# Three plain tiles share the input tiles as they come, and the first combined weights and inputs are made in another order

## What is computed

```python
def rms_norm(x, gain):
    y = xf * lax.rsqrt(jnp.mean(xf * xf, axis=-1, keepdims=True) + NORM_EPS)
    return (y * gain.astype(jnp.float32)).astype(x.dtype)

def swiglu(xn, w_in, w_out):          # 1024 -> 2 x 2816 -> 1024
    gate, up = jnp.split(xn @ w_in, 2, axis=-1)
    return (jax.nn.silu(gate) * up) @ w_out

x = first_block(x, ...)      # FFN 0, two-branch attention, FFN 1, then a norm of the result
x = second_block(x, ...)     # FFN 2, stick-breaking attention, FFN 3
# in either block: x = x + 0.5 * swiglu(rms_norm(x, n1), wi1, wo1), mixer, the same again
```

## Time and profile before

| | |
|---|---|
| median of 3 runs | 2038.31 us (2038.15 to 2039.38) |
| profiled execution, its own time | 2038.09 us |
| its span | 2036.3 us |
| mean granted clock of PE | 0.996 |
| instructions in the trace | 33055 |

### The profile page before, as it was taken

One profiled execution on the slowest core, in us unless ns is written; L12 is line 12 of the kernel. 1 busy time (PEld: TensorE's weight loads), 2 busy tenths in 40 slices (PEclk: granted clock), 3 DMA queues, 4 the chain that ended last, 5 costly groups with the idle time before them and its releaser, 6 DMA issues. The chain is left out here.

```text
span 2036.3 us, 33055 instructions
## 1 busy us (share of the span) xinstructions
PE 2014.3 (99%) x12322; PEld 1769.7 (87%) x12322; DVE 1285.5 (63%) x2245; ACT 1068.1 (52%) x1767; POOL 1074.5 (53%) x704
## 2 busy tenths in 40 slices
PE   9999999999999999999998999999999998999999
PEld 6998998777778889989987998998878877998997
DVE  8752765667762577626767764665688867752762
ACT  6652654344443466525656652653677755642651
POOL 2764775433322448646744774775322335764863
PEclk9999999999999999999999999999999998999999
DMA  4232323322121223332232333333444422332322
GB/s 170 94 107 90 110 96 117 137 83 73 63 73 62 93 83 107 108 109 94 92 106 79 111 102 104 100 100 115 115 136 125 132 86 73 104 114 83 108 98 96
DMA packets 69086, 206.18 MB, mean 101 GB/s; under 512 B 8448, under 2 KB 9472, under 8 KB 68928
## 3 DMA queue, kind: packets, MB, share of 16 engines
q1 hardware_dynamic: 67520, 201.29, 30.2%
q10 hardware_dynamic: 1408, 2.78, 0.4%
HBM read 189.49 MB, written 2.10 MB: 94 GB/s over the span
## 5 line engine op out<-in xcount | busy, mean ns | idle before, releaser
L622 POOL TENSOR_TENSOR w_lo<-raw,w_hi 128x1024 fp32r<-128x1024 f32 (+2 forms) x232 | 471.8, 2043 | 693.0 <-ACT w_hi L1240 528.3
L1240 ACT ACTIVATE w_hi<-raw 128x512 fp32r<-128x512 f32 (+2 forms) x472 | 359.1, 765 | 313.9 <-PE ps L698 250.9
L633 POOL TENSOR_TENSOR w_lo<-s,w_hi 128x512 fp32r<-128x512 f32 x234 | 312.1, 1335 | 184.8 <-ACT w_hi L1240 183.1
L770 PE MATMUL ps<-t_hi,w_hi 128*128 128x256 f32 x1248 | 353.9, 284 | 2.6 <-DVE scratch L1922 2.2
L771 PE MATMUL ps<-t_lo,w_hi 128*128 128x256 f32 x1248 | 353.5, 283 | 0.0
L772 PE MATMUL ps<-t_hi,w_lo 128*128 128x256 f32 x1248 | 353.5, 283 | 0.0
L633 POOL TENSOR_TENSOR w_lo<-raw,w_hi 128x512 fp32r<-128x512 f32 x234 | 301.7, 1303 | 69.0 <-ACT w_hi L1240 68.9
L696 PE MATMUL ps<-xn_hi,w_hi 128*128 128x512 f32 x648 | 262.3, 405 | 10.3 <-issue 5.4
L770 PE MATMUL ps<-xn_hi,w_hi 128*128 128x256 f32 x936 | 265.3, 283 | 1.5 <-POOL w_lo L633 1.5
L772 PE MATMUL ps<-xn_hi,w_lo 128*128 128x256 f32 x936 | 265.1, 283 | 0.0
L771 PE MATMUL ps<-xn_lo,w_hi 128*128 128x256 f32 x936 | 265.1, 283 | 0.0
(11 more groups left out here) (259 smaller groups left out, 3779.5 us busy)
## 6 DMA issues: line engine op xcount, KB each, us to landing
raw<-weights SPq DMA_DIRECT2D x294, 512.0 KB, 3.3
raw<-weights SPq DMA_DIRECT2D x68, 256.0 KB, 2.8
raw<-weights SPq DMA_DIRECT2D x32, 384.0 KB, 3.0
k_hi_twice<-sb_k_hi SPq DMA_DIRECT2D x31, 128.0 KB, 2.3
k_lo_twice<-sb_k_lo SPq DMA_DIRECT2D x31, 128.0 KB, 2.3
x_sb<-x_t SPq DMA_DIRECT2D x8, 256.0 KB, 5.8
bias<-rel ACTq DMA_DIRECT2D x1, 2048.0 KB, 8.8
q_both<-sb_q_hi SPq DMA_DIRECT2D x16, 128.0 KB, 2.2
```

The costliest lines, as they stand in the source:

```text
L622: nc.gpsimd.tensor_tensor(w_lo[s][:, 0:tiles, :], raw[s][:, 0:tiles, :], w_hi[s][:, 0:tiles, :].bitcast(F32), ALU.subtract).then_inc(S["lo ...
L633: nc.gpsimd.tensor_tensor(quad_of(n, i, w_lo), factor(n, F, i, raw, s_sum), quad_of(n, i, w_hi).bitcast(F32), ALU.subtract).then_inc(S["q_ ...
L770: pe.matmul(to, w[0][:, k, :], hi, start=opens, stop=False, skip_group_check=True)
L1240: return nc.scalar.activation(dst, src, ACT.Copy)
```

## The change

- **FFN 0**: DVE and ACT put the gates and the hidden values of the plain tiles 0 and 1 ahead of most combined inputs.
- **Tails before FFN 1, 2 and 3** (DVE): `split_t1` and `split_t` of a tile stand one tile later, behind the next tile's update.
- **FFN 2 and 3** (PE): units (0,0), (0,1) and (1,0) (tile, half) go through the input tiles together: 12 matmuls of each for tiles 0 to 3, then the three share tiles 4, 5, 6 and 7, and the mean is taken in the fourth unit after its first block. Before, the mean stood behind seven blocks of the first unit and one of the second, ahead of the first unit's last block. Two PSUM banks are swapped for it.
- **FFN 1 to 3**: the first combined weights on ACT and DVE are interleaved with the hidden values of plain tile 0; `copy_c` now stands ahead of silu. The seven products wait for `rms_done` rather than for the last gate.
- **ahead**: in FFN 2 both further units are rounded before the first norm; before FFN 3 the third unit is rounded ahead of the tail of tile 7.
- **Mixer of block 2** (DVE): from tile 4 on, the update of tile k+1 stands ahead of the tail of tile k.

```diff
@@ plain_banks
-    ... else [(weights_bank(n), S2_BANK), (2, 3)][F]
+    ... else [(weights_bank(n), S2_BANK), (3, 2)][F]
@@ PE, up_in_seven
-                    pe.wait_ge(S["gate_scaled"], FT * n + first - 1)
+                    if n == 0:
+                        pe.wait_ge(S["gate_scaled"], first - 1)
+                    else:
+                        pe.wait_ge(S["rms_done"], FFN_STAT[n] + 1)
@@ PE, plain_tiles, n = 2 and 3
-            for g, k0, k1 in ((0, 0, UK - 1), (1, 0, 1), (0, UK - 1, UK), (1, 1, UK)):
-                one(0, g, waits if g == 0 else None, (k0, k1))
-            one(1, 0)
-            one(1, 1)
+            one(0, 0, waits, (0, QUAD))
+            one(0, 1, None, (0, QUAD))
+            updated(FFN_RES[n][0] - 1, tile_before_in(n, plain_banks(n, 1)[0]))
+            one(1, 0, None, (0, QUAD))
+            for k in range(QUAD, UK - 1):
+                for F, g in ((0, 0), (0, 1), (1, 0)):
+                    one(F, g, waits if F + g == 0 else None, (k, k + 1))
+            pe.wait_ge(S["xn_lo_done"], DT * FFN_INPUT[n] + DT)
+            for F, g in ((0, 0), (0, 1), (1, 0)):
+                one(F, g, None, (UK - 1, UK))
+            one(1, 1, lambda k: means(FFN_STAT[n]) if k == MEAN_AT else None)
@@ ACT, plain_tiles, n = 1 to 3
-            ahead(u)
+            if n < 3:
+                ahead(u)
+            if n > 1:
+                ahead(u + 1)
             first_norm(FFN_STAT[n])
-            ahead(u + 1)
+            if n == 1:
+                ahead(u + 1)
...
+            round_7(n, F, 1)
+            copy_c(n, F)
             silu(n, 0)
+            copy_a(n, F)
+            round_7(n, F, 5)
             round_h(n, 0)
-            first_weights(n)
+            round_7(n, F, 6)
+            round_7(n, F, 2)
@@ DVE, tail
                 if k < QUAD:
                     make_t1(m, k)
-                    split_t1(m, k)
                 elif k < QUAD + T_IN_TAIL[m]:
                     make_t(m, k - QUAD)
-                    split_t(m, k - QUAD)
+                if 1 <= k <= QUAD:
+                    split_t1(m, k - 1)
+                elif QUAD < k <= QUAD + T_IN_TAIL[m]:
+                    split_t(m, k - QUAD - 1)
@@ DVE, plain_tiles, n = 0
-                for k in range(2):
-                    make_t1(0, k)
-                    make_t(0, k)
+                make_t1(0, 0)
                 dve.wait_ge(S["rstd_ready"], S_START + 1)
                 plain_gate(0, 0)
                 plain_gate(0, 1)
...
@@ DVE, plain_tiles, n = 1 to 3
                 plain_gate(n, 0)
+                sum_1(n, PLAIN[n])
+                sum_3(n, PLAIN[n])
                 plain_h(n, 0)
+                sum_2(n, PLAIN[n])
                 split_h(n, 0)
+                rest_of_6(n, PLAIN[n])
+                plain_gate(n, 1)
+                plain_h(n, 1)
+                split_h(n, 1)
+                return
@@ DVE, end of the mixer of block 2
-            for k in range(4):
+            for k in range(DT):
+                if 4 <= k + 1 < DT:
+                    update(k + 1, LAST_BANK[k + 1], update_from(k + 1), 1.0, MIX_RES[1], None, None, None)
                 tail(k, k % 2, T_MIX2, S_MIX2)
-            for k in range(4, DT):
-                update(k, LAST_BANK[k], update_from(k), 1.0, MIX_RES[1], T_MIX2, S_MIX2, k % 2)
+MEAN_AT = 1
```

More of the change, by code:

```diff
@@ L167, in plain_banks @@
 def plain_banks(n, F):
-    return [(0, 1), (2, 3), (BANK_OF_2, BANK_OF_2 + 1), (2, 3)][F] if n == 0 else [(weights_bank(n), S2_BANK), (2, 3)][F]
+    return [(0, 1), (2, 3), (BANK_OF_2, BANK_OF_2 + 1), (2, 3)][F] if n == 0 else [(weights_bank(n), S2_BANK), (3, 2)][F]
 def down_bank(n, k):
@@ L714, in mean_square, with means @@
               .then_inc(S["ms_done"], 1)
+        def means(stat):
+            mean_square(stat)
+            if stat == S_FINAL:
+                pe.wait_ge(S["sum_lo_done"], SUMS[stat] + 1)
+                pe.matmul(PS[:, 7, :], mean_all_r[:, :], sum_hi[1][:, :], start=True, stop=False)
+                pe.matmul(PS[:, 7, :], mean_all_r[:, :], sum_lo[1][:, :], start=False, stop=True)\
+                  .then_inc(S["ms2_done"], 1)
         def first_unit_waits(t, stat):
             def before(k):
-                if k == mean_at(stat):
+                if k == mean_at(stat) and stat not in (S_FINAL, S_MIX2):
                     mean_square(stat)
[L722 to L726, removed]
                 pe.wait_ge(S["xn_lo_done"], DT * t + k + 1)
@@ L854, in plain_tiles @@
             updated(FFN_RES[n][0] - 1, 1)
-            for g, k0, k1 in ((0, 0, UK - 1), (1, 0, 1), (0, UK - 1, UK), (1, 1, UK)):
-                one(0, g, waits if g == 0 else None, (k0, k1))
-            one(1, 0)
-            one(1, 1)
+            if n == 1:
+                for g, k0, k1 in ((0, 0, UK - 1), (1, 0, 1), (0, UK - 1, UK), (1, 1, UK)):
+                    one(0, g, waits if g == 0 else None, (k0, k1))
+                one(1, 0)
+                one(1, 1)
+                return
[10 more added lines that the diff above has]
+            one(1, 1, lambda k: means(FFN_STAT[n]) if k == MEAN_AT else None)
         def ffn(n):
@@ L1397, in make_xg @@
               .then_inc(S["xg_made"], 1)
[L1399 to L1406, removed]
         def plain_tiles(n):
@@ L1422, in plain_tiles @@
                 round_h(0, 0)
-                round_t1(0, 0)
-                round_t(0, 0)
                 round_h(0, 1)
-                for k in range(1, QUAD):
-                    if k == QUAD - 1:
+                for k in range(QUAD):
+                    round_t1(0, k)
+                for k in range(QUAD):
+                    if k == 2:
                         silu(0, 2)
-                    round_t1(0, k)
                     round_t(0, k)
                 round_h(0, 2)
-                first_weights(0)
+                round_7(0, PLAIN[0], 1)
+                copy_c(0, PLAIN[0])
+                copy_a(0, PLAIN[0])
+                for i in (5, 6, 2):
+                    round_7(0, PLAIN[0], i)
                 silu(0, 3)
@@ L1731, in mixer_2 @@
                     ahead(U_FFN4 + 1 - AHEAD)
+                if k == DT - 1:
+                    ahead(U_FFN4)
                 tail(k, k % 2, MIX_RES[1], T_MIX2, S_MIX2)
@@ L2555, in mean_at, with tile_before_in @@
     return {S_FFN1: 6, S_FFN3: 5}.get(stat, DT - 1)
+def tile_before_in(n, bank):
+    return LAST_BANK.index(bank) if n == 3 else [down_bank(n - 1, k) for k in range(DT)].index(bank)
+MEAN_AT = 1
 def mean_bank(stat):
```

19 lines of the change are left out of this document (12 added, 7 removed).

## The result

| | median, us | runs | ratio to before (95% interval) |
|---|---|---|---|
| before | 2038.32 | 4 (2038.15 to 2039.38) | |
| changed | 2050.64 | 4 (2050.25 to 2051.32) | 1.006 (1.0042 to 1.0077) |

A forecast was written before the change was run, and what follows sets the result against it. PE was taken to bound the kernel, busy 2014.3 of 2036.3 us. The FFN terms -1.3 + 0.9 + 14.8 - 0.3 = +14.1 on 2038.1 gave 2052 us, range 2043 to 2060.

The forecast's parts named there:

- FFN 0: FFN 0: PE's 3.36 us wait and slow stretch go, first combined weights come last; -1.3 us, bounds 0 and -2.5.
- FFN 1: Tail before FFN 1: split_t ahead of tile 7's update delays the mean; +0.9 us, bounds 0 and +2.5.
- FFN 2, the third unit: FFN 2: unit ready near 1092.5, PE stands some 6.5 us, then 1.6 us of slow clock.
- FFN 2, the mean: FFN 2: mean at 1105.7, before 1087.97; late product at 1129.9, before 1115.13, so +14.8 us.
- 8.0 from mean to gate: FFN 2: chain from mean at 1105.7 to gate at 1113.7 takes 8.0 us, before 13.65.
- "16.2" from gate to late product: FFN 2 and 3: copy_c, silu's table load, copy_a and a handover lengthen this way from 13.5 to 16.2 us.
- FFN 3: FFN 3: mean near 1697.7, before 1690.02, takes the gain of removed waits; -0.3 us, bounds -2.5 and +2.6.
- What PE would be seen to wait for: FFN 2: several us of PE idle between fourth unit and late product, put down to DVE or ACT steps.
- The first rival: Whole kernel: the sharing covers the waits in FFN 0, 2 and 3; -13.8, about 2024 us; chance 0.09.
- The third rival: FFN 0, 2 and 3: loss and gains cancel, FFN 2's chain 5 us shorter; +2, about 2040; chance 0.06.

The follow-up runs named there:

- e5: Changed kernel with DVE's splits of the combined inputs back ahead of the next tile's update in the tails before FFN 1 and 2: 2046.79 us.
- e1: Changed kernel with the third weight unit of FFN 2 rounded on ACT ahead of the tail of tile 7: 2042.03 us.
- e7: Changed kernel with FFN 3's mean behind 45 matmuls in place of 75: 2048.12 us.
- e4: Changed kernel with the first combined weights of FFN 1 to 3 made in the order of before on ACT and DVE: 2051.96 us.
- e2: Changed kernel with FFN 2's mean ahead of the third unit, behind 24 matmuls in place of 75: 2036.98 us.
- e11: e10 with the second unit of FFN 3 rounded on ACT ahead of the tail of tile 4 instead of tile 5: 2034.86 us.
- e10: Changed kernel with FFN 2's old PE order, the edits of e5 and e7, and FFN 3's first gate ahead of the four splits on DVE: 2030.88 us.

## Why the prediction was right

2050.64 us lies in the range, 1.4 us from the 2052 predicted, and the sign, the place (FFN 2) and the mechanism (a late third unit, then a late mean whose chain nothing covers) were right. That the total comes so close is in part luck: in FFN 2 and in FFN 3 two errors of nearly 4 us each cancel. The steps:

- **FFN 0**: the wait and the slow stretch went as said, and the chain of the first weights took part of it back. The size is -2.0 to -2.5 over the runs, the term was -1.3 with bounds 0 and -2.5.
- **FFN 1**: +0.8 for +0.9, and undoing the deferral brings it to 0 (e5). Shown.
- **FFN 2, the third unit**: my times were on the clock of the kernel before, and the changed kernel is 1.2 us ahead of it when FFN 2 begins. With these 1.2 us added, the third unit is in use at 1092.4, where I had it ready at 1092.5, and update 7 is at 1084.35 for my 1084.7; PE stood 6.34 for my 6.5. That DVE was blocked there was argued before and is shown by e5. One thing I had not seen: I took the block as given by the POOL step's place and priced the deferral at a net gain in the tail (-1.8 and +0.96). In fact the deferral itself brought the block about, and costs 3.4 us in FFN 2.
- **FFN 2, the mean**: 1106.8 on the clock of before, for 1105.7. The 1.1 us are the slow clock behind the wait, 2.75 us where I had 1.6. From the mean to the late product 24.1 us, for 24.2, and the chain has this length wherever nothing covers it: 24.1 in e1, e5 and e7 as well, and 24.2 in e4, with the old order of the first weights. But this total hides two errors against each other. From the mean to the gate took 11.7 us (1105.58 to 1117.32), not 8.0: two splits of the combined inputs (1.8 us) stand on DVE ahead of it, and `rstd` itself met a POOL step (1.75 us). From the gate to the late product took 12.3, not 16.2: the copy and the uncovered table load are real (1118.12 to 1120.04), but they lay beside the sums of the first weights, which DVE made in that time and which before came behind the hidden value. That this is the reason is argued from the order; that the way is not longer is measured. **The two terms that failed** are the 8.0 from mean to gate and the "16.2" from gate to late product; on the second, e4 shows the interleaving at about zero in FFN 2 and a gain of 1.2 us in FFN 3.
- **FFN 3**: -1.3 for -0.3. The mean came at 1711.13, which is 1696.6 on the clock of before (14.5 us later by then), for my 1697.7, and that the late mean eats the gain is shown by e7. The same two errors stand here: from the mean to the gate I had 0.9 + 1.35, and it took 6.3 (1711.13 to 1717.39), because the four splits (3.56 us) stand ahead of the gate on DVE, as in the kernel before; from the gate to the late product I had 16.2, and it took 12.3. Together 18.6 for 18.45.
- **What PE would be seen to wait for**: I had put the idle time ahead of the late product down to DVE or ACT steps. The rows name POOL's `w_lo`, which is the last step in making the first weights; ahead of it stand ACT's list behind the norm and the gate.
- **The first rival** (the sharing covers the waits) held in the tails: no wait for `xn_lo` is left. It failed where it said what would decide: the chain from the mean is 24 us, not 12.
- **The third rival** was added up wrongly: by its own terms it gives -2.5 + 0.9 + 9.8 - 2.5 = +5.7, not +2.

Of the Trainium skill's two rules, the one on blocking ("SBUF — State Buffer", section "Who interferes with whom") is borne out: in e5 the update with a PSUM operand ran at 0.68 us beside a POOL step, and in the changed kernel `xn_lo` with two SBUF operands took 2.88. The rule on table loads ("ScalarE: Activation LUTs", section "What ACT_TABLE_LOAD costs") would add a drain of 1.4 us; behind the gate silu starts 0.02 us after the end of the load's 1.28 us, so no drain shows here, and the measurement decides.

## What to carry to other kernels

When PE is 99% busy and its waits are named, look for the longest chain that starts at a PE instruction and returns to PE, and keep that instruction as early as its inputs allow, however the waits around it are filled: taking four matmuls of a mean from behind 75 to behind 24 gained 13.7 us (e2), and the waits of the earlier trace rows that the reordering removed were 9.3 us together. Test a reordering stage by stage: compare one and the same matmul in both traces at the quiet places between stages; that splits a sum of +13 into -2, +1, +16 and -1 in one view. And where DVE and POOL both work in SBUF, an edit that brings a POOL step forward by 1 us can land it on another DVE operation: 1.2 us sooner made tile 7's update 2.8 us late in the changed kernel, and 1.15 us sooner cost 4 us in e11.

## What I had not expected of the hardware

**The clock after a wait.** In the changed kernel PE runs at the 1.2 GHz level for 5.7 us behind the 6.34 us wait in the profiled execution. In e7, with the same code in FFN 2 and the same wait, the mean granted clock over the same stretch is 0.75, so about half of it was at 2.4 GHz. The stretch just before, in which PE stood still, is the other way round: 0.92 in the changed kernel and 0.68 in e7, so that there the clock had fallen earlier, while PE had nothing to do. Columns as in the earlier trace rows; the changed kernel, then e7:

```profile
1085.00:1091.00 6.00, 0.00 (x0) 0.00 (x0) 5.64 (x7) 5.67 (x8) 2.48 (x1) 0.92 0.01 1
1091.20:1096.90 5.70, 5.68 (x14) 4.50 (x15) 3.93 (x5) 0.00 (x0) 2.38 (x1) 0.50 0.56 184
```

```profile
1085.00:1091.00 6.00, 0.00 (x0) 0.00 (x0) 5.81 (x7) 5.50 (x8) 2.65 (x2) 0.68 0.00 1
1091.20:1096.90 5.70, 5.70 (x20) 4.60 (x21) 3.77 (x4) 0.00 (x0) 2.21 (x1) 0.75 0.51 184
```

The first 18 matmuls behind the wait took 6.85 us in the changed kernel and 5.57 in e7; at full clock they take 4.1 (18 x 0.2275). That is the 1.3 us by which the two differ in FFN 2 (15.7 and 14.4). The changed kernel's four times span 1.1 us. So a wait of this size cost 6.3 us and another 1.5 or 2.75, with the same code. Why the clock falls earlier in one execution than in another isn't shown.

**Where a POOL step falls decides, not how long it is.** The same POOL step of 2.4 us cost DVE 2.1 us in the changed kernel (2.88 for 0.74) and 0.2 at most in e5, by the operation that it fell on. In e11 and e10 it cost DVE 1.7 and 1.6 us, and yet e11 is 4 us slower, since there more waits behind the blocked operation.
